# Grouped attention turned tile by tile: one burst of transposes into three banks, then the value products, then the scores

## The reference, cut to what matters

```
s = einsum('bqkgd,bnkd->bkgqn', q_blk, k) * scale      # scores, f32
p = softmax(s, axis=-1)
o = einsum('bkgqn,bnkd->bqkgd', p, v)                  # value products
y = (o * silu(g)) @ w_out
```

## Time and profile before

| what | value |
|---|---|
| median of three runs | 1786.4 us |
| the profiled execution | 1790.98 us, span 1788.9 us |
| TensorE busy over the span | 1622.4 us, 91% |
| VectorE busy, ScalarE busy | 799.0 us, 782.9 us |
| this stage, first score to last product | 415.7 to 752.3 us |
| mean granted TensorE clock | 0.958 of full speed |

### The profile page before, as it was taken

One profiled execution on the slowest core, in us unless ns is written; L12 is line 12 of the kernel. 1 busy time (PEld: TensorE's weight loads), 2 busy tenths in 40 slices (PEclk: granted clock), 3 DMA queues, 4 the chain that ended last, 5 costly groups with the idle time before them and its releaser, 6 DMA issues. The chain is left out here.

```text
span 1788.9 us, 26339 instructions
## 1 busy us (share of the span) xinstructions
PE 1622.4 (91%) x9936; PEld 1398.4 (78%) x9936; DVE 799.0 (45%) x1866; ACT 782.9 (44%) x1802; POOL 310.7 (17%) x331
## 2 busy tenths in 40 slices
PE   7799999998999999899999998999958998779876
PEld 3177778897899999788788886899847887778764
DVE  1612211216888888644323322102136675556551
ACT  4211222216777777655512212112136775567551
POOL 0202110001222111100200000046003332223220
PEclk9899999999999999999999999999969998899888
DMA  7456411317111540142155576253399877787852
GB/s 279 145 165 187 122 45 51 123 64 228 29 21 22 157 157 16 55 127 82 59 175 155 176 210 197 101 171 93 92 256 256 238 239 209 197 224 201 220 127 59
DMA packets 188177, 256.17 MB, mean 143 GB/s; under 512 B 33954, under 2 KB 144116, under 8 KB 188020
## 3 DMA queue, kind: packets, MB, share of 16 engines
q1 hardware_dynamic: 185876, 246.10, 46.8%
q10 hardware_dynamic: 2176, 8.39, 2.0%
HBM read 193.62 MB, written 76.66 MB: 151 GB/s over the span
## 5 line engine op out<-in xcount | busy, mean ns | idle before, releaser
L2017 DVE CUSTOM_DVE_ANT_0 nprob<-nS,bias_sets 128x640 f32<-128x640 f32 x128 | 105.4, 823 | 171.4 <-PE nS L1879 85.7
L1483 PE MATMUL p<-h_hi,w_hi 128*128 128x512 f32 (+1 forms) x448 | 169.4, 378 | 10.2 <-ACT g_stage L1597 4.2
L1484 PE MATMUL p<-h_lo,w_hi 128*128 128x512 f32 (+1 forms) x448 | 168.8, 377 | 0.0
L1485 PE MATMUL p<-h_hi,w_lo 128*128 128x512 f32 (+1 forms) x448 | 168.5, 376 | 0.0
L600 PE MATMUL pp<-h_hi,w_hi 128*128 128x512 f32 (+1 forms) x432 | 157.1, 364 | 8.6 <-PEq L124 8.6
L1959 ACT CAST npt_hi<-nTB 128x256 fp32r<-128x256 f32 (+1 forms) x256 | 100.1, 426 | 144.5 <-PE nTB L1890 143.6
L601 PE MATMUL pp<-h_lo,w_hi 128*128 128x512 f32 (+1 forms) x432 | 154.0, 356 | 0.0
L602 PE MATMUL pp<-h_hi,w_lo 128*128 128x512 f32 (+1 forms) x432 | 154.0, 356 | 0.0
L1109 ACT ACTIVATE prob<-S,nm,qk_inv 128x512 f32<-128x512 f32 (+1 forms) x208 | 146.3, 706 | 8.3 <-DVE nm L1045 8.3
L1063 DVE TENSOR_TENSOR ptlo<-TB,pthi 128x512 fp32r<-128x512 f32 (+1 forms) x192 | 114.7, 598 | 29.7 <-ACT pthi L1121 27.9
L1121 ACT CAST pthi<-TB 128x512 fp32r<-128x512 f32 (+1 forms) x192 | 99.2, 517 | 63.1 <-PE TB L990 62.7
(11 more groups left out here) (228 smaller groups left out, 4306.6 us busy)
## 6 DMA issues: line engine op xcount, KB each, us to landing
kq_scratch<-p_stage SPq DMA_DIRECT2D x96, 256.0 KB, 4.0
kq_strip<-kq_scratch SPq DMA_DIRECT2D x32, 768.0 KB, 6.4
bias_sets<-bias_scratch SPq DMA_DIRECT2D x64, 384.0 KB, 8.3
v_strip<-v_scratch SPq DMA_DIRECT2D x128, 128.0 KB, 3.1
wmod<-in_mod_w SPq DMA_DIRECT2D x24, 512.0 KB, 4.5
wside<-in_mod_w SPq DMA_DIRECT2D x12, 1024.0 KB, 5.0
bias_scratch<-bias_wide_scratch SPq DMA_DIRECT2D x16, 768.0 KB, 10.9
w_raw<-in_na_w_in SPq DMA_DIRECT2D x11, 1024.0 KB, 7.7
```

What stands on the lines that cost most here:

```text
L1483: pe.matmul(ps[:, bank, 0:width], whi[:, k, ws], hi[:, k, a:a + width], start=(k == 0), stop=False)
L1484: pe.matmul(ps[:, bank, 0:width], whi[:, k, ws], lo[:, k, a:a + width], start=False, stop=False)
L1485: last = pe.matmul(ps[:, bank, 0:width], wlo[:, k, ws], hi[:, k, a:a + width], start=False, stop=(k == KT - 1))
```

## The change

The order inside a step is by kind of work and no longer by chunk. TensorE turns all chunks of tile p-3, then does the products of the step, then all scores of tile p. ScalarE does all `high`, then all `exps`. VectorE does all `low`, then `out`, then all `biggest`. `TB` has three banks, one for each chunk index, and a turn waits until the last tile that had such a chunk has been subtracted (`turned_before`). `S` has four banks in place of five, taken in turn through all heads. No instruction that computes is added or removed.

```diff
-S_RING = 5
+S_RING = 4
-def score_bank(p, k):
-    return (3 * (p % GQA_N) + k) % S_RING
+def score_bank(h, p, k):
+    return (h * CHUNKS + chunk_no(p, k)) % S_RING
...
-        S, TB, O = c.ps("S", [P, S_RING, 512]), c.ps("TB", [P, 2, 512]), c.ps("O", [P, 512])
+        S, TB, O = c.ps("S", [P, S_RING, 512]), c.ps("TB", [P, 3, 512]), c.ps("O", [P, 512])
...
+        def turned_before(p, k):
+            q = p - 1
+            while len(key_chunks(q)) <= k:
+                q -= 1
+            return chunk_no(q, k)
... TensorE
-                    at_least(pe, expd, CHUNKS, h, bank_user_before(p, k))
+                    at_least(pe, expd, CHUNKS, h, chunk_no(p, k) - S_RING)
...
-                    at_least(pe, lod, CHUNKS, h, no - 2)
+                    at_least(pe, lod, CHUNKS, h, turned_before(p, k))
...
+                        for k in range(len(turns)):
+                            turn(h, q, k)
                         for k in range(3):
-                            if k < len(turns):
-                                turn(h, q, k)
-                            if k < len(chunks):
-                                scores(h, kv, p, k)
                             if live(gr, prev, tail):
                                 product(h, kvp if gr < 0 else kv, gr, (p - PRODUCT) % 2, k)
+                        for k in range(len(chunks)):
+                            scores(h, kv, p, k)
... VectorE
-                        for k in range(3):
-                            if k == 0 and (p - OUT) % 2 == 0 and live((p - OUT) // 2, prev, tail):
-                                out(h, (p - OUT) // 2)
-                            if k == 2 and k < len(chunks):
-                                biggest(h, p, k)
-                            if k < len(turns):
-                                low(h, q, k)
-                            if k < len(chunks) and k < 2:
-                                biggest(h, p, k)
+                        for k in range(len(turns)):
+                            low(h, q, k)
+                        if (p - OUT) % 2 == 0 and live((p - OUT) // 2, prev, tail):
+                            out(h, (p - OUT) // 2)
+                        for k in range(len(chunks)):
+                            biggest(h, p, k)
... ScalarE
-                        for k in range(3):
-                            if k < len(turns):
-                                high(h, q, k)
-                            if k < len(es):
-                                exps(h, p - 1, k)
+                        for k in range(len(turns)):
+                            high(h, q, k)
+                        for k in range(len(es)):
+                            exps(h, p - 1, k)
```

More of the change, by code:

```diff
@@ L976, in scores @@
                         at_least(pe, q_lo, 3, h, (0, 4, 8).index(p))
-                    at_least(pe, expd, CHUNKS, h, bank_user_before(p, k))
-                    acc = S[:, score_bank(p, k), 0:n]
+                    at_least(pe, expd, CHUNKS, h, chunk_no(p, k) - S_RING)
+                    acc = S[:, score_bank(h, p, k), 0:n]
                     qs = slice(tok, tok + P)
@@ L987, in turn @@
                     at_least(pe, expd, CHUNKS, h, no)
-                    at_least(pe, lod, CHUNKS, h, no - 2)
+                    at_least(pe, lod, CHUNKS, h, turned_before(p, k))
                     for b in range(n // P):
-                        last = pe.transpose(TB[:, no % 2, b * P:(b + 1) * P],
+                        last = pe.transpose(TB[:, k, b * P:(b + 1) * P],
                                             prob[:, p % 5, a + b * P:a + (b + 1) * P], consts["ident"][:, :])
@@ L1037, in biggest @@
                     at_least(dve, qkd, CHUNKS, h, chunk_no(p, k))
-                    dve.tensor_reduce(mx[:, p % 5, k:k + 1], S[:, score_bank(p, k), 0:n], AX, ALU.max).then_inc(mxd, 1)
+                    dve.tensor_reduce(mx[:, p % 5, k:k + 1], S[:, score_bank(h, p, k), 0:n], AX, ALU.max).then_inc(mxd, 1)
                 def negmax(h, p):
@@ L1062, in low @@
                     blocks = slice(a // P, (a + n) // P)
-                    dve.tensor_tensor(lo[:, blocks, :], TB[:, no % 2, 0:n].rearrange("p (b q) -> p b q", q=P),
+                    dve.tensor_tensor(lo[:, blocks, :], TB[:, k, 0:n].rearrange("p (b q) -> p b q", q=P),
                                       hi[:, blocks, :], ALU.subtract).then_inc(lod, 1)
@@ L1108, in exps @@
                         at_least(act, td, CHUNKS, h, chunk_no(p - 5, len(key_chunks(p - 5)) - 1))
-                    act.activation(prob[:, p % 5, a:a + n], S[:, score_bank(p, k), 0:n], ACT.Exp,
+                    act.activation(prob[:, p % 5, a:a + n], S[:, score_bank(h, p, k), 0:n], ACT.Exp,
                                    bias=nm[:, p % 5:p % 5 + 1],
@@ L1121, in high @@
                     act.copy(hi[:, a // P:(a + n) // P, :],
-                             TB[:, no % 2, 0:n].rearrange("p (b q) -> p b q", q=P)).then_inc(hid, 1)
+                             TB[:, k, 0:n].rearrange("p (b q) -> p b q", q=P)).then_inc(hid, 1)
                 def body(h, kv, kvp, tail=False):
```

## The result

The changed kernel takes 1928.6 us in the median of four runs (1923.9 to 1929.8) against 1785.3 us before: 1.079 times as long, 95% interval 1.076 to 1.082. The forecast was 1939 us, range 1880 to 1990. The profiled execution is 1928.3 us, span 1926.2 us.

A forecast was written before the change was run, and what follows sets the result against it. TensorE's own instruction list plus its waits was taken to bound the stage. Stops before the products 105 us, score banks 5.5 and clock 42 summed to 153 us; against the 1786.4 us median that gave 1939 us, range 1880 to 1990.

The forecast's parts named there:

- The list costs the same: TensorE's instructions in the stage: a turn costs 0.11 us however many stand together, so a burst saves 0.
- Block 0 behind the lows: Odd steps: TensorE's first product waits for `out`, now behind three `low` on VectorE; full stop 3.07 us, 105 us in all.
- Fewer score banks: With four banks `scores(p,1)` waits for the previous tile's first exponential, mainly in step 4 and head 0's first steps; 5.5 us.
- ScalarE's lateness: Rival: if ScalarE is late, score banks make each step of tiles 1 to 7 wait; 50 us more, 1989 us, chance 0.05.
- The clock: TensorE's clock falls to half after three in four of 37 new pauses, 1.5 us each; 42 us.
- the first term: The stops of TensorE before the products, with `out` behind the lows on VectorE; 105 us of the sum.
- The clock did not hold: Rival that TensorE's clock holds: the pauses come and no more, 1897 us, chance 0.15.
- did not fall for longer than 3.4 us: Rival: TensorE's clock falls at each pause and for long, 5.3 us of work; 1995 us, chance 0.07.
- Score banks did not bind in every full step: Rival: each step of tiles 1 to 7 waits up to 0.9 us for score banks; 1989 us, chance 0.05.
- The stop was shorter than forecast: Rival: TensorE's stop before the products is say 2 us, as VectorE overlaps better; 1850 to 1880 us, chance 0.06.
- The 0.09 us after a turn group: Rival, faster: the first matmul after turns pays 0.09 us for switching, so fewer switches win 15 us; 1771 us, chance 0.02.

## Why the prediction was right, step by step

**The list costs the same.** Right. Ten turns in a burst bring nothing: 328.7 us busy with them (with `out` in the even step), 329.0 without, and ten turns with no wait behind them take 1.09 us there.

**Block 0 behind the lows.** The mechanism was right and 105 us were too many. The idle time before the first products grew by 94.9 - 5.4 = 89.5 us. A full step has 3.81 us from first turn to first product; I had 4.22. Two terms were mis-sized. `low(0)` starts at 1.25, not 1.40: the three maxima (538.22, 1.71 us) are done sooner, so the start is the one that I had for `high(0)` as releaser. The three lows take 1.54 us from first start to the copy's start (540.32 to 541.86), not 1.80. I had taken the recorded length of three maxima in a row for them. In the changed kernel the three lows together are recorded as 1.62, and the next starts 0.08 before that ends. For TensorE I had subtracted starts; for VectorE I had not. The last link, `out` until TensorE goes on, was right: 1.02 us from 541.86 to 542.88. (A slip besides: 4.22 less 1.1 is 3.12, where the prediction has 3.07; under 2 us in all.)

**Fewer score banks.** 5.5 us were priced, and the waits for exponentials rose from 0.2 to 6.9 us, 6.7: 0.5 in step 4 of each of seven heads, as forecast, and 3.5 in the first steps of head 0, where I had 1.5. Right, also in that the cover is the products: take the burst order away and the same banks cost 32 us, take away one bank more and it is 24.4 us of waits. That the banks were the second largest risk of the design I had not seen. I gave ScalarE's lateness one chance in twenty, for this order rightly.

**The clock.** 42 us forecast, 44 measured by filling the pauses. It fell at 30 of 37 pauses, where I took three in four, and each fall cost 1.5 us. The share was a guess from two cases in four, so that it came out is partly luck; the price per fall was worked out. Almost all of the 3.4 us fell on work, at most 0.6 of them into the pause. The rule of the Trainium skill ("TensorE: Matmul & The Clock Gate", "HAM oscillation — how this bites in real kernels"), that gaps between bursts of matmuls bring the clock down again and again, is what this trace shows, at 30 of 37 pauses. By that rule as I had read it, each pause would count; seven did not. The waits in that section's example, 3 to 5 us for a DMA, are also longer than the stops here (2.2 to 2.6 us recorded), so I had stretched it.

**Sum.** 89.5 + 6.7 + 44 = 140 us, against 143.1 in the stage. The 3 us are within what the record can tell: from first turn to first product it is 3.81 us with the wait and 1.09 without, so a full stop is 2.72 us where the idle time says 2.56, and over 37 stops that makes some 6 us. The forecast's 153 was 10 over: the first term, mostly the lows and what stands ahead of them, was 15 too high, and the others together were 5 too low, which brought the sum nearer than its parts.

**The rivals.** The clock did not hold and did not fall for longer than 3.4 us. Score banks did not bind in every full step. The stop was shorter than forecast, but 2.7 us by starts and not 2. The 0.09 us after a turn group was indeed no price of switching, since ten switches a head in place of 31 changed no busy time (328.7 against 329.0). The kernel was not faster.

No version here beats the kernel before. The one with `out` in the even step comes nearest, 0.1 to 0.5% behind. To order ScalarE by turns in steps 3 and 4 alone, where the products are short, was not tried.

## What to carry to other kernels

When work is grouped by kind, ask of each single-buffered tile where its release now stands in the other engine's queue. Here one instruction pair behind three others, in a bank that TensorE wants next, cost 95 us; in the step in which its input becomes ready it cost next to nothing. And a pause of TensorE can have two prices: its length, and here, at 30 pauses of 37, 1.5 us more for 3.4 us at half clock.

## What was not expected of the hardware

- Two instructions of VectorE that read a bank one after the other start 0.33 us apart at 256 columns, though each is recorded as 0.41; the multiplication that waits for the copy starts 0.45 after it. A chain is summed from starts.
- 342 useless matmuls, some 80 us of TensorE's time at 0.235 each, made the kernel 44 us faster, for they kept the clock at 0.99.
